# Hybrid encoder step on one core: level-0 masks on VectorE, state-space scaling moved between the delta rule's last solves, first output weights in a free slot

## Chip, cores and metric

One core of a Trainium2 chip. The time is that of one execution of the whole program on the device, in microseconds; the number that counts is the median of several runs. All stretches in the text are on the clock of one profiled execution, counted from the start of its span.

## What is computed

A two-layer encoder step in fp32 over 288 rows: 256 frames of a new stream ("prompt") and 32 frames of a running one ("sample"). Layer 0's mixer runs state-space heads and gated delta-rule heads side by side; layer 1's mixer is another recurrence; each mixer is followed by a mixture of 32 experts. Cut to what the change touches:

```python
def gdn_block(s_mat, inp):                       # delta rule, one block of rows
    ...
    a_mat = (beta[:, :, None, :] * dec_strict * jnp.einsum('bthk,bshk->btsh', k, k)).transpose(0, 3, 1, 2)
    eg = jnp.exp(gam)
    rhs = beta[..., None] * (v - eg[..., None] * jnp.einsum('bthk,bhkv->bthv', k, s_mat))
    u = lax.linalg.triangular_solve(a_mat + jnp.eye(l), rhs, left_side=True, lower=True, unit_diagonal=True)
    qk = jnp.einsum('bthk,bshk->bhts', q, k) * dec_incl.transpose(0, 3, 1, 2)
    o = jnp.einsum('bhts,bhsv->bthv', qk, u) + eg[..., None] * jnp.einsum('bthk,bhkv->bthv', q, s_mat)
    tail = jnp.exp(gam[:, -1:, :] - gam)
    s_new = s_mat * jnp.exp(gam[:, -1])[:, :, None, None] + jnp.einsum('bshk,bsh,bhsv->bhkv', k, tail, u)

def ab_mixer(...):
    ...
    y = rms_norm(y * silu(z_s), by 2 groups)               # state-space half, 1024 channels
    o = rms_norm(o, w['gdn_norm'][j]) * jax.nn.silu(z_g)   # delta-rule half, 1024 channels
    mix = jnp.concatenate([y, o], axis=-1) @ w['w_out_ab'][j]
```

## The kernel before

The 288 rows are three tiles of 128, 128 and 32 rows (tiles 0 and 1 are the prompt, tile 2 the sample). Each engine has its own program written out by hand, and semaphores order them; each runs its program strictly in order. SP issues the transfers, also in order.

The stage around the change comes behind the state-space heads. For each tile the delta rule's triangular matrix is inverted by levels: VectorE cuts the 32-wide diagonal blocks into a compact matrix (`gdn_mats`, L1127), GpSimd masks it for level 0 and, in one operation, for levels 1 to 4 (`gdn_masked`, L523 and L525), TensorE does level 0 (`gdn_first`, L1692) and for each further level a product (L1708, L1715) and an update (L1727 to L1737), with copies on ScalarE (`gdn_p`) and sums on VectorE (`gdn_level`). GpSimd further scales the far blocks (`gdn_far`, L537, L539), copies diagonal blocks (`gdn_blocks`) and makes two side products, the scaled queries and keys (`gdn_sides`, L551, L552). The levels of the three tiles are interleaved by hand on every engine. Then per tile TensorE does a product with the known state (`gdn_known`, L1751), a solve (`gdn_solve`, L1767) and an output with the state's update (`gdn_output`, L1783 to L1787); VectorE makes the right-hand side (`gdn_rhs`), scales the solution (`gdn_solved`) and updates the state (`gdn_state`); ScalarE copies the output out of PSUM (`gdn_out`, L771).

The state-space half waits meanwhile in `cat[:, 0:8]`. TensorE sums its squares (L1845) between `gdn_known(2)` and `gdn_output(1)`, ScalarE takes the root, and VectorE scales the half by the root and by a weight (`ssd_scale`, two operations over 128 x 2304) as its last step of the stage, behind `gdn_state(2)`. Then `head_norm` normalises the delta-rule half in three rounds of heads: ScalarE squares (L814), TensorE sums (`round_sums`, L1858), ScalarE roots, VectorE scales. The output projection (`project_out`, L1890, L1895) takes 16 chunks of 128 channels in four groups of four, each with 2 MB of weights: groups 0 and 1 are the state-space half, groups 2 and 3 the delta-rule half. The weights come into three ring slots, which hold delta-rule data before, so SP loads them behind the last state store (L404 to L411). VectorE adds the result to the residual; then the expert stage begins, whose first expert's weights SP loads once the mixer's output is complete (`cat_ready` 3).

```python
            gdn_update(2, 4)
            gdn_solve(1)
            gdn_known(2)
            ...
            gdn_output(1)
            gdn_solve(2)
            gdn_output(2)
```

Of the kernel before, what the change touches and what calls it, by code (L numbers as in the profile page):

```python
# [8 lines left out]
P = 128  # L9
KD = D_MODEL // P  # L10
TILES = 3
# [16 lines left out]
GROUP = 512  # L28
# [16 lines left out]
SUB = 32  # L45
INNER = 5
# [33 lines left out]
def build(nc, ins, outs):  # L80
# [9 lines left out]
    with ctx:  # L90
# [8 lines left out]
        xn = sb("xn", [P, TILES, D_MODEL])  # L99
# [90 lines left out]
        for three in (gDQK, gDKK):  # L190
            three.append(take(cur, SSD_DEAD, 8, SUB))
        gQ2 = take(cur, SSD_DEAD, 8, SUB)
# [23 lines left out]
        gKtok = in_uT_early(4, P)  # L216
# [119 lines left out]
        for name in ("x_loaded consts_loaded h_ready sq_done xn_ready xnT_ps uT_ready dve_step act_step "  # L336
                     "proj_ps proj_evac conv_out conv_act small_ps small_evac sp_exp1 sp_pos sp_ln g_ready "
                     "ea_ready cum_ps cum_ready pool_step ssd_in ssd_diff ssd_exp ssd_w ssd_y ssd_upd st_T st_Tevac z_act "
                     "state_in ssd_final yg_ready sq2_done nrm_ps nrm_done gdn_in gdn_diff gdn_exp gdn_mats "
                     "gdn_gb gdn_vt gdn_c gdn_far gdn_dqk gdn_copied gdn_masks "  # L340
                     "gdn_bm gdn_p gdn_pe gdn_pt gdn_tu gdn_ks gdn_rhs gdn_u gdn_ue gdn_o gdn_upd gdn_out "
                     "state_loaded gdn_vb gdn_side cat_ready out_ps out_loaded0 out_loaded1 out_loaded2 "
                     "states_out conv_new_ready beta_ready ring0 ring1 ring2 decay_in decay_act hg_keep hg_d "
                     "hg_e hg_qk hg_att hg_acc hg_in hg_x hg_y hg_ex hg_upd hg_tr hg_out lg_ps rt_diff rt_exp "
                     "rt_A rt_R rt_OH rt_tab route_done xn_stored xg_zero xgathered weight_ready "
                     "xg_T xT_ready wg0 wg1 wg2 wu0 wu1 wu2 wd0 wd1 wd2 gu_ps sg_ready hid_ready "
                     "hT_ps hidT_ready y_ps y_ready placed_ps h_added y_out hist_loaded ss_set small_loaded "
                     "final_loaded rs_done").split():
            s_(name)
# [19 lines left out]
        def _(sp):  # L369
# [32 lines left out]
            for n, name in enumerate(("gdn_p", "gdn_s")):  # L402
# [4 lines left out]
            def load_out(src, groups, first):  # L407
                for g in range(groups):
                    if g >= 3:
                        sp.wait_ge(S["out_ps"], first + g - 2)  # L410
                    sp.dma_start(ring[g % 3].rearrange("p a b -> p (a b)").rearrange("p (c d) -> p c d", c=4),  # L411
                                 src[g * 4 * P:(g + 1) * 4 * P, :].rearrange("(c p) d -> p c d", p=P)
                                 ).then_inc(S[f"out_loaded{g % 3}"], 16)

            sp.wait_ge(S["yg_ready"], 2)
            load_out(ins["w_out_ab"], 4, 0)
# [41 lines left out]

            sp.wait_ge(S["cat_ready"], 3)
# [16 lines left out]
            load_out(ins["w_out_c"], 2, 4)  # L476
# [16 lines left out]
        def _(pool):  # L493
# [34 lines left out]

            def gdn_far(i):

                s = i % 2
                nb = lambda q, w: gNb[q, i].unsqueeze(2).to_broadcast([w, 8, w])
                pool.wait_ge(S["gdn_mats"], i + 1)
                pool.wait_ge(S["gdn_bm"], 2 * i + 2)
                for r in (0, 2):
                    q, c = slice(SUB * r, SUB * r + SUB), slice(SUB * r + SUB, SUB * r + 2 * SUB)
                    p(G.tensor_tensor(gDKK[s][q, :, c], gDKK[s][q, :, c], nb(q, SUB), ALU.mult))  # L537
                q, c = slice(0, 2 * SUB), slice(2 * SUB, P)
                G.tensor_tensor(gDKK[s][q, :, c], gDKK[s][q, :, c], nb(q, 2 * SUB), ALU.mult).then_inc(S["gdn_far"], 1)  # L539

            def gdn_sides(i):
# [4 lines left out]
                if i:  # L546
                    pool.wait_ge(S["gdn_copied"], i)
                else:
                    pool.wait_ge(S["gdn_far"], 1)
# [3 lines left out]
                                gKtok[0:L].unsqueeze(2).to_broadcast([L, 4, 2, P]),  # L553
# [3 lines left out]
            def gdn_blocks(i):  # L557
# [3 lines left out]
                if i:  # L561
                    pool.wait_ge(S["gdn_bm"], 6)
                else:
                    pool.wait_ge(S["gdn_far"], 2)
# [61 lines left out]
        def _(act):  # L626
# [290 lines left out]
        def _(dve):  # L917
# [209 lines left out]
            def gdn_mats(i):  # L1127
# [10 lines left out]
                c_.then_inc(S["gdn_c"], 1)  # L1138

# [366 lines left out]
        def _(pe):  # L1506
# [178 lines left out]
            def gdn_first(i):  # L1685

                pe.wait_ge(S["gdn_bm"], 2 * i + 1)
# [7 lines left out]
            def gdn_product(i, n):  # L1695
# [3 lines left out]
                if n == 1:  # L1699
                    pe.wait_ge(S["gdn_bm"], 2 * i + 2)  # L1700
# [138 lines left out]
            gdn_solve(1)  # L1839
            gdn_known(2)  # L1840

# [4 lines left out]
            m_.then_inc(S["nrm_ps"], 1)  # L1846
            gdn_output(1)
# [31 lines left out]
            round_sums(0, 0)  # L1879

            def project_out(src, groups, first, between):
                for g in range(groups):
                    pe.wait_ge(S[f"out_loaded{g % 3}"], 16 * out_use(first, g))
                    w = ring[g % 3].rearrange("p a b -> p (a b)").rearrange("p (c d) -> p c d", c=4)
# [14 lines left out]
            pe.wait_ge(S["nrm_done"], 3)  # L1899
            project_out(cat, 4, 0, out_steps_0)  # L1900
# [197 lines left out]
def inv_step(i, n):  # L2098

    return INVERSE.index((i, n))  # L2100
# [108 lines left out]
```

## Time and profile before

| | us |
|---|---|
| median of 3 runs | 1781.13 (1779.69 to 1784.95) |
| the profiled execution, its own time | 1776.18 |
| its span, first to last instruction | 1774.4 |
| TensorE matmuls busy | 1253.9 (71%) |
| VectorE busy | 453.2 (26%) |
| ScalarE busy | 371.4 (21%) |
| GpSimd busy | 65.5 (4%) |

PE is TensorE's matmuls, PEld its weight loads, DVE VectorE, ACT ScalarE, POOL GpSimd, SPq the transfers that SP issues. An element-wise VectorE operation shows line 928, that of a helper, so tensors and shapes tell which one it is. `ps` is PSUM; `arena`, `uT`, `xn` and `cvt` are SBUF. Most matmuls are fp32 and show as two records each. The clock is the share of full TensorE speed that the chip granted. Busy shares are means over stages with different limits; what a stage is worth is read from the chain in that stage.

### The profile page before, as it was taken

How to read it: one execution, taken by the hardware profiler on the slowest of the kernel's cores; microseconds unless marked ns; L12 is line 12 of the kernel's file. 1: busy time of each engine (PE TensorE's matmuls, PEld its weight loads, DVE VectorE, ACT ScalarE, POOL GpSimd, SP SyncE). 2: the span in 40 equal slices, each digit the busy share in tenths (PEclk: the TensorE clock that was granted, in tenths of full speed). 3: DMA queues.
4: the chain of work that ended last, by engine and by line, in shares of the span. 5: the costliest groups of instructions: out<-in, count | busy, mean ns of one | idle time of the engine just before them, and what ended most of it. 6: DMA issues, size and time to landing. Idle time of an engine off the chain costs nothing.

```text
span 1774.4 us, 26723 instructions
## 1 busy us (share of the span) xinstructions
PE 1253.9 (71%) x12028; PEld 830.3 (47%) x12028; DVE 453.2 (26%) x819; ACT 371.4 (21%) x756; POOL 65.5 (4%) x69
## 2 busy tenths in 40 slices
PE   6999976869747556646665799988466655664664
PEld 5777766844434233323332578774343323332332
DVE  3546444320241011101100248611511101110111
ACT  3352121131102111111111233523121111111112
POOL 0000023100000000000000001100000000000000
PEclk9999986759769788888888899988688888788888
DMA  6333010036469999999999141033879999999993
GB/s 251 105 133 109 1 37 4 2 116 239 172 250 423 420 421 419 421 419 420 420 422 411 59 142 48 1 119 113 351 279 421 421 422 420 420 421 419 421 420 152
DMA packets 72540, 473.23 MB, mean 267 GB/s; under 512 B 5600, under 2 KB 15072, under 8 KB 53600
## 3 DMA queue, kind: packets, MB, share of 16 engines
q1 hardware_dynamic: 70112, 466.68, 64.7%
q0 software_dynamic: 2304, 4.72, 0.8%
q8 instruction: 99, 1.62, 0.4%
q14 instruction: 25, 0.20, 0.0%
HBM read 468.28 MB, written 6.77 MB: 268 GB/s over the span
## 4 chain that ended last, share of the span: by engine, by line
PE 51%; DMA 30%; DVE 7%; SPq 5%; issue 3%; ACT 2%; DVEq 0%; POOL 0%; ACTq 0%; POOLq 0%
DMA arena<-in_wu 25%; PE ps L1530 16%; PE ps L1940 9%; SPq L428 5%; PE ps L1890 5%; PE ps L1969 4%; DMA arena<-in_wg 4%; DVE arena L928 3%; PE ps L1959 2%; PE ps L2046 1%; DVE h L928 1%; PE ps L1518 1%; PE ps L1906 1%; PE ps L1895 1%; PE ps L1567 1%
## 5 line engine op out<-in xcount | busy, mean ns | idle before, releaser
L1530 PE MATMUL ps<-uT,arena 128*128 128x288 f32 x1216 | 306.8, 412 | 0.8 <-DVE uT L928 0.8
L1940 PE MATMUL ps<-arena,xn 128*32 128x256 f32 x2048 | 167.0, 496 | 154.7 <-issue 116.0
L1530 PEld LDWEIGHTS ps<-uT,arena 128*128 128x128 f32 x1216 | 232.6, 193 | 66.1 <-issue 2.2
L1940 PE MATMUL ps<-arena,uT 128*32 128x256 f32 x2048 | 163.3, 487 | 122.9 <-issue 87.1
L928 DVE TENSOR_TENSOR uT<-uT,ps 64x256 f32<-64x256 f32 (+1 forms) x72 | 30.2, 424 | 746.1 <-ACT uT L834 677.9
L1940 PEld LDWEIGHTS ps<-arena,xn 128*32 128x32 f32 x2048 | 90.3, 141 | 233.7 <-issue 218.1
L1940 PEld LDWEIGHTS ps<-arena,uT 128*32 128x32 f32 x2048 | 91.9, 139 | 194.5 <-issue 178.2
L1959 PE MATMUL ps<-arena,uT 128*32 128x256 f32 x2048 | 125.2, 385 | 21.6 <-issue 18.6
L843 ACT ACTIVATE xn<-ps 32x256 f32<-32x256 f32 x256 | 95.9, 374 | 199.3 <-PE ps L1959 106.9
L834 ACT ACTIVATE uT<-ps 64x256 f32<-64x256 f32 x64 | 24.0, 375 | 494.6 <-PE ps L1940 494.6
L1969 PE MATMUL ps<-xn,uT 128*128 128x512 f32 (+1 forms) x192 | 92.9, 609 | 18.9 <-DVE h L928 15.6
L928 DVE TENSOR_TENSOR h<-h,ps 128x1024 f32<-128x1024 f32 (+2 forms) x60 | 66.3, 1110 | 148.0 <-PE ps L1969 91.8
L1959 PEld LDWEIGHTS ps<-arena,uT 128*32 128x32 f32 x2048 | 69.7, 110 | 63.6 <-issue 34.3
L1890 PE MATMUL ps<-arena 128*128 128x512 f32 x192 | 87.7, 614 | 3.8 <-DMA arena<-in_w_out_ab 3.8
L928 DVE TENSOR_TENSOR arena<-arena 128x512 f32<-128x512 f32 (+7 forms) x108 | 76.0, 747 | 52.1 <-ACT arena L637 22.1
L1890 PEld LDWEIGHTS ps<-arena 128*128 128x128 f32 x192 | 37.6, 198 | 50.4 <-issue 49.8
L1969 PEld LDWEIGHTS ps<-xn,uT 128*128 128x128 f32 (+1 forms) x192 | 28.7, 162 | 58.2 <-issue 33.8
L1948 PE MATMUL ps<-con,uT 64*128 64x64 f32 x128 | 21.4, 247 | 38.9 <-DVE uT L928 38.9
L1518 PE MATMUL ps<-con,xn 128*128 128x128 f32 (+1 forms) x96 | 18.4, 373 | 41.2 <-DVE xn L939 41.2
L1948 PEld LDWEIGHTS ps<-con,uT 64*128 64x128 f32 x128 | 12.6, 137 | 68.6 <-DVE uT L928 56.2
L1022 DVE SCALAR_TENSOR_TENSOR cvt<-arena,vec,cvt 128x291 f32<-128x291 f32 x84 | 43.9, 523 | 3.0
L2046 PE MATMUL ps<-arena 128*128 128x128 f32 (+1 forms) x352 | 39.0, 270 | 7.6 <-DVE arena L928 7.6
(328 smaller groups left out, 1175.5 us busy)
## 6 DMA issues: line engine op xcount, KB each, us to landing
arena<-in_wg SPq DMA_DIRECT2D x64, 2048.0 KB, 34.3
arena<-in_wu SPq DMA_DIRECT2D x64, 2048.0 KB, 31.0
arena<-in_wd SPq DMA_DIRECT2D x64, 2048.0 KB, 34.7
arena<-in_wA SPq DMA_DIRECT2D x11, 2048.0 KB, 8.4
arena<-in_wC SPq DMA_DIRECT2D x8, 2048.0 KB, 8.7
arena<-in_w_out_ab SPq DMA_DIRECT2D x4, 2048.0 KB, 10.2
arena<-in_w_out_c SPq DMA_DIRECT2D x2, 2048.0 KB, 12.6
xn_rows<-xn SPq DMA_DIRECT2D x4, 512.0 KB, 15.3
```

What stands on the lines that cost most here:

```text
L428: sp.dma_start(dst, src).then_inc(signals[name], 16)
L843: y_ = nc.scalar.activation(yb[SLOTS * q:SLOTS * (q + 1), 256 * g:256 * (g + 1)], ps[SLOTS * g:SLOTS * (g + 1), 5, 0:256], ACT.Copy)
L928: return V.tensor_tensor(out, a, b, op)
L1022: op = V.scalar_tensor_tensor(out, xpad[:, t, j:j + XW], wv(j), out, ALU.mult, ALU.add)
L1518: t_ = nc.tensor.transpose(bank(4 + k % 4, 4, P)[:, j, 0:L], xn[0:L, i, 4 * c + j::KD], ident[0:L, 0:L])
L1530: m_ = MM(ps[:, banks[t % len(banks)], 0:TOK], ring[s][:, k, (t % 4) * P:(t % 4 + 1) * P], uT[:, k, :], start=(k == 0), stop=(k == KD - 1))
L1890: MM(ps[:, 2 * i + n, :], src[:, k, AT[i]:AT[i] + P], w[:, c, 512 * n:512 * n + 512], start=(k == 0), stop=(k == 4 * groups - 1))
L1940: m_ = MM(ps[SLOTS * g:SLOTS * (g + 1), 2 + n % 2, 0:H2], x[:, k, SLOTS * q:SLOTS * (q + 1)], w[s][:, k, H2 * (g % 2):H2 * (g % 2 + 1)], s ...
L1948: t_ = nc.tensor.transpose(bank(4, 2, 2 * SLOTS)[:, m, :], hid[2 * SLOTS:, m * P:(m + 1) * P], ident[2 * SLOTS:, 2 * SLOTS:])
L1959: m_ = MM(ps[SLOTS * g:SLOTS * (g + 1), 5, 0:n_], hidT[:, m, SLOTS * src:SLOTS * (src + 1)], wdb[s][:, k, n_ * g:n_ * (g + 1)], start=(k = ...
L1969: m_ = MM(ps[0:L, b + g, 0:n_], weight[:, AT[t]:AT[t] + L], yb[:, n_ * g:n_ * (g + 1)], start=True, stop=True)
L2046: m_ = MM(bank(step_bank(m), 8, P, n=2)[0:L, hd, 0:L], a_, b_, start=True, stop=True)
```

## The change

- The level-0 mask moves from GpSimd to VectorE, right behind the compact matrix; GpSimd keeps levels 1 to 4. A new semaphore `gdn_b0` releases `gdn_first`.
- GpSimd's program is reordered: the mask of tile 1 waits for the far blocks of tile 0, the mask of tile 2 moves ahead of the side products of tile 0, and these ahead of the block copies of tile 1. The keys that the side products read get a second buffer, so ScalarE's copy no longer waits for the tile before.
- On TensorE the state-space sums move ahead of `gdn_solve(1)`; on VectorE `ssd_scale` moves ahead of `gdn_state(1)`.
- SP loads the first group of output weights into a slot of its own (`w_first`, over dead state-space data), once the last level and the side products are done; groups 1 and 2 once the last output is done; group 3 behind the last state store. Loading the first expert waits for group 0 to be used.
- The output projection starts without the first round of head sums; the rounds move to its chunks (0, 2), (1, 0) and (1, 2). It waits for the copy of the last delta-rule output.
- Two small tensors of tile 2 move to other free memory.

```diff
+        w_first = at(RING, KD, GROUP)
...
-        gKtok = in_uT_early(4, P)
+        gKtok = [in_uT_early(4, P), xn[:, 0, 0:512].rearrange("p (a b) -> p a b", a=4)]
...
+            sp.wait_ge(S["gdn_pe"], len(PRODUCTS))
+            sp.wait_ge(S["gdn_pt"], len(INVERSE))
+            sp.wait_ge(S["gdn_tu"], inv_step(1, INNER + 1) + 1)
+            sp.wait_ge(S["gdn_side"], TILES)
+            load_rows(w_first, ins["w_out_ab"], 0, S["out_loaded0"])
+            store_state(0, "gdn_p")
+            sp.wait_ge(S["gdn_o"], TILES)
+            load_rows(ring[1], ins["w_out_ab"], 1, S["out_loaded1"])
+            load_rows(ring[2], ins["w_out_ab"], 2, S["out_loaded2"])
+            store_state(1, "gdn_s")
             sp.wait_ge(S["states_out"], 16 * 6)
...
-            sp.wait_ge(S["yg_ready"], 2)
-            load_out(ins["w_out_ab"], 4, 0)
+            load_rows(ring[0], ins["w_out_ab"], 3, S["out_loaded0"])
...
+            sp.wait_ge(S["out_ps"], 1)
             sp.wait_ge(S["cat_ready"], 3)
             load_expert(0, 0, None, slots[0])
...
                 if i == 1:
+                    pool.wait_ge(S["gdn_far"], 1)
                     pool.wait_ge(S["states_out"], 64)
+                elif i == 2:
+                    pool.wait_ge(S["gdn_copied"], 1)
                 low = gDc[i][0:L].unsqueeze(1)
-                G.tensor_tensor(gB[i][0:L, 0:1], low, cmask[0:L, 0:1].unsqueeze(2).to_broadcast([L, 1, 8, SUB]), ALU.mult
-                                ).then_inc(S["gdn_bm"], 1)
                 G.tensor_tensor(gB[i][0:L, 1:INNER], low.to_broadcast([L, INNER - 1, 8, SUB]),
...
             gdn_masked(0)
             gdn_far(0)
-            gdn_sides(0)
             gdn_masked(1)
             gdn_far(1)
             gdn_blocks(0)
+            gdn_masked(2)
+            gdn_sides(0)
+            gdn_blocks(1)
             gdn_sides(1)
-            gdn_masked(2)
-            gdn_blocks(1)
             gdn_sides(2)
...
-                if i:
-                    act.wait_ge(S["gdn_side"], i)
-                nc.scalar.activation(gKtok[0:L], bank(7, 4, P)[0:L], ACT.Copy)
+                need(act, S["gdn_side"], i - 1)
+                nc.scalar.activation(gKtok[s][0:L], bank(7, 4, P)[0:L], ACT.Copy)
...
                 c_.then_inc(S["gdn_c"], 1)
+                dve.wait_ge(S["gdn_c"], i + 1)
+                if i == 0:
+                    dve.wait_ge(S["gdn_masks"], 1)
+                elif i == 1:
+                    dve.wait_ge(S["states_out"], 64)
+                tt(gB[i][0:L, 0], gDc[i][0:L], bc(cmask[0:L, 0].unsqueeze(1), 8, SUB), ALU.mult).then_inc(S["gdn_b0"], 1)
...
             gdn_rhs(2)
+            ssd_scale()
             gdn_state(1)
             gdn_solved(2)
             gdn_state(2)
-            ssd_scale()
...
             gdn_update(2, 4)
-            gdn_solve(1)
-            gdn_known(2)
-
+            pe.wait_ge(S["gdn_tu"], inv_step(1, INNER + 1) + 1)
             pe.wait_ge(S["sq2_done"], 3)
             for g in range(2):
                 for c in range(4):
                     m_ = MM(ps[:, g, 0:TOK], ones, Z[:, 4 * g + c, :], start=(c == 0), stop=(c == 3))
             m_.then_inc(S["nrm_ps"], 1)
+            gdn_solve(1)
+            gdn_known(2)
+
             gdn_output(1)
...
                 if (g, c) == (0, 2):
+                    round_sums(0, 0)
+                elif (g, c) == (1, 0):
                     round_sums(0, 1)
-                elif (g, c) == (1, 1):
+                elif (g, c) == (1, 2):
                     round_sums(0, 2)
...
-            round_sums(0, 0)
-
...
             pe.wait_ge(S["nrm_done"], 3)
+            pe.wait_ge(S["gdn_out"], TILES)
             project_out(cat, 4, 0, out_steps_0)
```

## Rows read from the trace of the kernel before

**Rows 1.** The first expert stage by stretch: length, busy time by engine, clock, DMA share.
```profile
core 0: us, PE busy (x) PEld busy (x) DVE busy (x) ACT busy (x) POOL busy (x), PEclk, DMA share, GB/s
467.00:960.00 493.00, 296.18 (x3372) 167.31 (x3372) 73.21 (x159) 72.58 (x195) 9.07 (x9) 0.80 0.98 403
```

**Rows 2.** The chain of waits of the whole run: start us, us, what.
```profile
376.06 3.72 PE ps L1787 x16
...
384.79 2.56 DVE arena L928
387.46 7.90 DMA arena<-in_w_out_ab
395.49 8.97 PE ps L1890 x16
...
463.07 2.67 DVE h L928 x3
```

**Rows 3.** GpSimd's timeline: start us, us, operation [idle before <-releaser].
```profile
263.93 2.18 POOL L551 TENSOR_TENSOR arena<-arena 128x1024 f32<-128x1024 f32 x1 [0.17 <-POOL arena L539]
266.07 1.90 POOL L552 TENSOR_TENSOR arena<-uT,arena 128x1024 f32<-128x1024 f32 x1
...
344.88 1.89 POOL L552 TENSOR_TENSOR arena<-uT,arena 32x1024 f32<-32x1024 f32 x1
```

**Rows 4.** DMA issues: count, KB each, median us from issue to landing.
```profile
arena<-in_w_out_ab SPq DMA_DIRECT2D x4, 2048.0 KB, 10.2
```

**Rows 5.** Timeline of TensorE, VectorE and ScalarE, tiles 1 and 2 up to the seam.
```profile
349.92 4.15 PE L1845 MATMUL ps<-arena,con 128*128 128x288 f32 x16
351.47 1.21 DVE L928 TENSOR_TENSOR arena<-arena 32x1024 f32<-32x1024 f32 x1
354.11 0.74 ACT L636 ACTIVATE xn<-ps,con 128x576 f32<-128x576 f32 x1 [8.70 <-PE ps L1845]
356.16 0.68 ACT L637 ACTIVATE xn<-xn 128x576 f32<-128x576 f32 x1
359.46 1.22 DVE L928 TENSOR_TENSOR arena<-arena 128x1024 f32<-128x1024 f32 x1 [6.78 <-PE ps L1787]
362.09 3.59 PE L1767 MATMUL ps<-arena 32*32 32x128 f32 x16 [2.66 <-DVE arena L928]
...
379.81 0.38 ACT L771 ACTIVATE arena<-ps 128x256 f32<-128x256 f32 x1 [15.88 <-PE ps L1787]
...
382.20 2.55 DVE L928 TENSOR_TENSOR arena<-arena,xn 128x2304 f32<-128x2304 f32 x1
```

**Rows 6.** Timeline of TensorE in the output projection: one round of head sums.
```profile
404.30 1.62 PE L1858 MATMUL ps<-uT,con 128*128 128x288 f32 x6
```

**Rows 7.** The chain of waits inside the delta-rule stage: start us, us, what.
```profile
255.99 0.73 POOL arena L523
...
325.24 1.98 PE ps L1783 x16
```

**Rows 8.** Timeline of VectorE and GpSimd around tile 0's masks.
```profile
254.13 1.71 DVE L928 TENSOR_TENSOR uT<-arena 32x256 f32<-32x256 f32 x4
256.67 2.34 POOL L525 TENSOR_TENSOR arena<-uT,cvt 128x1024 f32<-128x1024 f32 x1
257.91 0.42 DVE L928 TENSOR_TENSOR uT<-ps,cvt 128x256 f32<-128x256 f32 x1 [0.82 <-PE ps L1692]
258.25 1.04 DVE L928 TENSOR_TENSOR uT<-arena,cvt 128x256 f32<-128x256 f32 x1
```

**Rows 9.** Stretches of tile 1's end, the last solve and the projection, columns as in rows 1.
```profile
348.00:360.00 12.00, 11.43 (x81) 10.14 (x80) 4.34 (x5) 3.25 (x4) 0.00 (x0) 1.00 0.00 0
362.00:380.00 18.00, 16.37 (x64) 14.04 (x64) 1.41 (x2) 2.12 (x2) 0.00 (x0) 0.50 0.11 30
395.00:399.00 4.00, 3.51 (x4) 1.51 (x5) 2.18 (x2) 1.28 (x1) 0.00 (x0) 0.50 1.02 414
399.00:463.00 64.00, 64.00 (x263) 28.90 (x261) 3.75 (x4) 7.18 (x7) 0.00 (x0) 1.00 0.43 167
```

More of the change, by code:

```diff
@@ L189, in build @@
         compact = [None, [take(cur, SSD_DEAD, 8, SUB) for _ in range(4)], None]
-        for three in (gDQK, gDKK):
-            three.append(take(cur, SSD_DEAD, 8, SUB))
-        gQ2 = take(cur, SSD_DEAD, 8, SUB)
+        gDKK.append(take(cur, SSD_DEAD, 8, SUB))
+        in_xn = lambda at_: xn[:, 2, at_:at_ + 8 * SUB].rearrange("p (a b) -> p a b", a=8)
+        gDQK.append(in_xn(280))
+        gQ2 = in_xn(536)
+        w_first = at(RING, KD, GROUP)
         cur = [in_pad]
@@ L339, in build @@
                      "state_in ssd_final yg_ready sq2_done nrm_ps nrm_done gdn_in gdn_diff gdn_exp gdn_mats "
-                     "gdn_gb gdn_vt gdn_c gdn_far gdn_dqk gdn_copied gdn_masks "
+                     "gdn_gb gdn_vt gdn_c gdn_far gdn_b0 gdn_dqk gdn_copied gdn_masks "
                      "gdn_bm gdn_p gdn_pe gdn_pt gdn_tu gdn_ks gdn_rhs gdn_u gdn_ue gdn_o gdn_upd gdn_out "
@@ L401, in _, with load_rows, store_state @@
             sp.dma_start(GS[1], ins["st_gdn"].rearrange("h k v -> k h v")).then_inc(S["state_loaded"], 16)
-            for n, name in enumerate(("gdn_p", "gdn_s")):
+            def load_rows(dst, src, g, done):
+                sp.dma_start(dst.rearrange("p a b -> p (a b)").rearrange("p (c d) -> p c d", c=4),
+                             src[g * 4 * P:(g + 1) * 4 * P, :].rearrange("(c p) d -> p c d", p=P)).then_inc(done, 16)
+            def store_state(n, name):
                 sp.wait_ge(S["gdn_upd"], 2 + n)
                 sp.dma_start(outs[name].rearrange("h k v -> k h v"), GS[n]).then_inc(S["states_out"], 16)
-            sp.wait_ge(S["states_out"], 16 * 6)
[L407 to L413, printed above, removed]
-            sp.wait_ge(S["yg_ready"], 2)
-            load_out(ins["w_out_ab"], 4, 0)
+            sp.wait_ge(S["gdn_pe"], len(PRODUCTS))
[8 more added lines that the diff above has]
+            store_state(1, "gdn_s")
+            sp.wait_ge(S["states_out"], 16 * 6)
+            load_rows(ring[0], ins["w_out_ab"], 3, S["out_loaded0"])
             def load_expert(s, e, free, signals):
@@ L475, in _ @@
             sp.dma_start(hS[1], ins["st_hgrn"].rearrange("h k v -> k h v")).then_inc(S["state_loaded"], 16)
-            load_out(ins["w_out_c"], 2, 4)
+            for g in range(2):
+                load_rows(ring[g], ins["w_out_c"], g, S[f"out_loaded{g}"])
             for n, name in enumerate(("hgrn_p", "hgrn_s")):
@@ L533, in gdn_far @@
                 pool.wait_ge(S["gdn_mats"], i + 1)
-                pool.wait_ge(S["gdn_bm"], 2 * i + 2)
+                pool.wait_ge(S["gdn_bm"], i + 1)
                 for r in (0, 2):
@@ L546, in gdn_sides @@
                 if i:
-                    pool.wait_ge(S["gdn_copied"], i)
-                else:
-                    pool.wait_ge(S["gdn_far"], 1)
+                    pool.wait_ge(S["gdn_copied"], 2)
                 q4 = gQ[i].rearrange("p (a b) c -> p a b c", b=2)[:, :, :, 0:L]
@@ L552, in gdn_sides @@
                 G.tensor_tensor(gKt[s][0:L].rearrange("p (a b) c -> p a b c", b=2),
-                                gKtok[0:L].unsqueeze(2).to_broadcast([L, 4, 2, P]),
+                                gKtok[s][0:L].unsqueeze(2).to_broadcast([L, 4, 2, P]),
                                 gTail[i][0:L].rearrange("p (a b) -> p a b", b=2).unsqueeze(3).to_broadcast([L, 4, 2, P]),
@@ L561, in gdn_blocks @@
                 if i:
-                    pool.wait_ge(S["gdn_bm"], 6)
+                    pool.wait_ge(S["gdn_side"], 1)
                 else:
@@ L1685, in gdn_first @@
             def gdn_first(i):
-                pe.wait_ge(S["gdn_bm"], 2 * i + 1)
+                pe.wait_ge(S["gdn_b0"], i + 1)
                 if i == 0:
@@ L1699, in gdn_product @@
                 if n == 1:
-                    pe.wait_ge(S["gdn_bm"], 2 * i + 2)
+                    pe.wait_ge(S["gdn_bm"], i + 1)
                 if n == INNER:
@@ L1883, in project_out @@
                     pe.wait_ge(S[f"out_loaded{g % 3}"], 16 * out_use(first, g))
-                    w = ring[g % 3].rearrange("p a b -> p (a b)").rearrange("p (c d) -> p c d", c=4)
+                    w = (w_first if (first, g) == (0, 0) else ring[g % 3]).rearrange("p a b -> p (a b)").rearrange("p (c d) -> p c d", c=4)
                     for c in range(4):
```

## The prediction

> **What bounds the kernel now.** I read three views first: the chain of waits of the whole run, to see on which stage the end hangs; the same chain with the timeline in the delta-rule stage; and the stretches with the granted clock. A projection, a recurrent mixer and an expert stage follow one another twice. The first expert stage is a stream of weights: from 467 to 960 us the DMA engines are busy 0.98 of the time [rows 1]. It opens once the first mixer's residual is done (VectorE at 463.07 [rows 2]), so a microsecond saved before 463 should be a microsecond of the run, and one lost there likewise. All that the change touches lies between 250 and 463 us.
>
> There the reader is to see one seam. TensorE finishes the last delta-rule output at 379.78 (376.06 + 3.72). VectorE then updates the state and scales the state-space half, the last step of it 2.56 us from 384.79; a fetch of the output weights takes 7.90; and only at 395.49 does the output projection start [rows 2]. TensorE then works without a break to 463.
>
> **The change, part by part.** All sums are on the trace's clock.
>
> *The seam.* The scaling moves ahead of the last state updates, and the first 2 MB of weights get a place that is free earlier, so the 395.49 - 379.78 = 15.7 us between output and projection fall away. Three things must hold.
> - Weights: SP issues group 0 after four waits, of which GpSimd's third side product comes last, at 344.88 + 1.89 = 346.8 [rows 3]. The state store behind it on the queue waits for tile 1's update, which is later, so nothing is held up. A load takes 10.2 us in the median [rows 4]: there near 357, some 25 us early. Groups 1 and 2 are issued when the last output is done, near 381.5; group 1 is wanted behind group 0's matmuls and sums, near 401. Group 3 waits for the last state store and is wanted near 436. All hidden; group 0, if it were not, would cost the 7.90 again.
> - Scaling: 2.55 + 2.56 = 5.1 us [rows 2, 5]. VectorE idles 6.78 us ahead of tile 1's state update [rows 5], while output 1 runs. The root that it needs took ScalarE from 354.11 to 356.84 (356.16 + 0.68) behind the sums [rows 5]; with the sums two TensorE steps earlier it ends near 353. So scaling starts with output 1 and takes 5.1 against 5.4 us: hidden with 0.3 us to spare. Without that cover it would delay the update and the last solve, at most by its own length.
> - The projection gets a wait for ScalarE's copy of the last output out of PSUM: 0.38 us [rows 5], with the handoff +0.5. The rest of TensorE's program is queued behind it.
>
> *Head sums.* The first of three rounds stood in the seam and is now inside group 0. A round of six costs 1.62 us at full clock [rows 6], double that at half: +1.6, as the clock was up by then before. Its squares are ready 3.4 us after the last output (update 2.5, square 0.9), while two chunks of group 0 take 6.9 or more: no wait. The later rounds each get half a group or more for the root and norm before them. Nothing.
>
> *A cover that goes.* The state-space sums (4.15 us from 349.92) stood between the product with the known state and output 1. They hid VectorE's right-hand side of tile 2, two operations of 1.21 us of which the second ends at 351.47 + 1.21 = 352.68 [rows 5], and output 1 waits for it. The sums now stand ahead of solve 1. TensorE's work up to that point is the same, but output 1 meets the wait: 352.68 - 349.99 = +2.7. Solve 2 and output 2 are queued behind, so it all moves the seam.
>
> *Level-0 masks.* GpSimd's mask is a piece of the chain at all three tiles; the first of the three pieces, 0.73 us, stands for them [rows 7]. VectorE does that shape in 0.42 us [rows 8] and saves a handoff between engines: from the compact matrix (254.13 + 1.71 = 255.84) to the mask's end (256.72) 0.88 us become about 0.5. I take 0.35 a tile, -1.0 in all. The masks of levels 1 to 4 start up to 0.7 us earlier on GpSimd. Other bound: VectorE's mask shares its start with GpSimd's big one (2.34 us), and VectorE's add with both inputs in SBUF took 1.04 us beside that, 0.42 with one in PSUM [rows 8]; at 1.04 the masks cost 0.2 to 0.3 us a tile, +0.8. I stay with 0.42, since VectorE has the shorter way to its own result.
>
> The Trainium skill, SBUF — State Buffer, section "Who interferes with whom", says that a VectorE instruction with two SBUF inputs and a GpSimd instruction that reads SBUF exclude each other: the one that issues first runs, the other fully blocks. That speaks against this move. The trace agrees: the 1.04 us add ended at 259.29, just after GpSimd's mask at 259.01.
>
> *GpSimd's order.* Side products of tile 0 (2.18 + 1.90 us [rows 3]) now follow the mask of tile 2, near 308 to 312; output 0 wants them at 325.24 [rows 7]. Those of tile 1 follow the copies of tile 1 and end near 330; output 1 wants them at 357. The second key buffer takes a wait off ScalarE that bound nothing. Nothing; without these margins each would cost at most its own 4.1 us.
>
> *Clock.* TensorE was granted 1.00 (2.4 GHz) from 348 to 360, 0.50 (1.2 GHz) from 362 to 380 and still in the projection's first 4 us, then 1.00 [rows 9]. I take the same levels for the same work, so the projection keeps its slow start (4 us at half speed, 2 us lost). Bounds: a start at full clock gives 2.0; output 1, which now starts after 2.7 us of idling, costs at half clock up to its 5.4 us again.
>
> **Sum.** -15.7 + 0.5 + 1.6 + 2.7 - 1.0 = -11.9 us. The profiled execution took 1776.18 us (span 1774.4), so it would be 1764.3. It lies 5 us below the median of the runs, 1781.13 (1779.69 to 1784.95); the same difference on the median gives **1769.2 us**.
>
> **Rivals.**
> - *Half clock at output 1.* For it: after the idle 2.66 us before solve 2 at 362.09 [rows 5] the clock was down for 18 us [rows 9], and the new gap is as long. Against it: the new gap stands behind 5 us or more of dense matmuls. Between nothing and 5.4 us, say 4: -7.9, 1773.2. Chance 0.17.
> - *GpSimd gets in first.* One VectorE operation releases both masks; if GpSimd's large one starts first and holds VectorE's for its 2.34 us, the mask of tile 0 ends near 258.7 instead of 256.72. Some +2.0 for -0.35 at each tile, +7.0 in all: -4.9, 1776.2. For it: the 1.04 us add. Against it: GpSimd started 0.15 us after the compact matrix, and VectorE follows itself in some 0.03. Chance 0.12. The skill's rule in the section named above makes this the case in which GpSimd issues first.
> - *The change does not reach the seam*: the projection still meets the 7.90 us fetch, -4.0, 1777.1. For that SP would have to stand somewhere behind 347 for 30 us; I find no such wait. Chance 0.04.
> - *Slower: the projection stays at half clock.* For it: from 362 to 380 TensorE was busy 16.37 of 18 us and got 0.50 all the same [rows 9], and the projection now follows straight on. Against it: after 4 us of the same matmuls it had 1.00. A microsecond at half clock loses half of one, so the gain is gone once the low stretch lasts 4 + 2 x 11.9 = 28 us. If two groups (15.8 us each at full clock) run so: +31.6 - 2.0 - 11.9 = +17.7, 1798.8. Chance 0.03.
>
> **How the numbers follow.** The forecast has what is left, 0.64. Its own bounds are 1769.2 - 2.0 (start at full clock) - 1.4 (the lowest run under the median) = 1765.8 and 1769.2 + 1.8 (masks at +0.8) + 1.4 = 1772.4. The range goes on to the clock rival and to GpSimd's, and a little lower for a clock that also stays up in solve 2: 1764.0 to 1776.5. A measurement of this kernel tells 0.3%, 5.3 us, from no change. Faster than 1775.8: the forecast, the clock rival and part of GpSimd's, 0.86. Within 5.3 us: the rest of that and the unreached seam, 0.11. Slower: the projection at half clock, 0.03.
>
> **What would show it.** Right: the first projection matmul less than 1 us after the last output matmul; group 0's weights issued near 347; both scaling operations beside output 1; some 2.7 us of idle TensorE ahead of output 1, released by VectorE; masks of 0.42 us on VectorE; the residual near 451 instead of 463. Wrong: masks of 2 us or more; group 0's first matmul released by a transfer; a group that takes 28 us; an expert stage of more than its 493 us [rows 1], which would give the gain back.

## The result, and the profile after

The changed kernel was timed three times, each time beside the kernel before on the same chip:

| measurement | changed, us: median (range, runs) | before, us | ratio, 95% interval |
|---|---|---|---|
| first | 1766.22 (1763.03 to 1768.73, 4) | 1780.46 | 0.9910 [0.9894, 0.9927] |
| second | 1770.62 (1766.16 to 1779.38, 12) | 1781.26 | 0.9941 [0.9926, 0.9957] |
| third | 1770.16 (1765.45 to 1776.37, 8) | 1781.98 | 0.9942 [0.9920, 0.9963] |

It is faster by 14.2, 10.6 and 11.8 us; the forecast of 11.9 us is a ratio of 1769.2 / 1781.13 = 0.9933. The first profiled execution after the change took 1767.64 us (span 1765.8, granted clock 0.845), against 1776.18 (span 1774.4).

**The seam.** The chain of waits of the changed kernel (start us, us, what), where [rows 2] had 15.7 us between output and projection:

```profile
383.09 3.71 PE ps L1802 x16
386.80 0.52 issue
387.31 8.84 PE ps L1906 x16
396.16 1.46 PE ps L1874 x6
397.61 6.87 PE ps L1906 x16
...
454.29 1.91 PE ps L1911 x32
456.20 0.02 issue
456.22 2.67 DVE h L937 x3
```

L1802 is the last output's state update, L1906 the projection: 0.52 us lie between them, which is the handoff with ScalarE's copy. The first round of head sums (L1874) stands inside group 0 and waits for nothing. The residual starts at 456.22 instead of 463.07.

**Tile 1's end, output 1, the last solve.** Timeline of the changed kernel, all engines, picked rows in order of time (start us, us, engine, line, operation; in brackets the idle time before it and what ended it):

```profile
348.23 6.62 PE L1858 MATMUL ps<-arena,con 128*128 128x288 f32 x16
348.76 1.89 POOL L562 TENSOR_TENSOR arena<-uT,arena 32x1024 f32<-32x1024 f32 x1
350.74 0.38 SPq L406 DMA_DIRECT2D arena<-in_w_out_ab  x1
354.69 1.95 PE L1782 MATMUL ps<-arena 128*128 128x128 f32 x16
356.56 1.93 PE L1766 MATMUL ps<-arena 128*32 128x128 f32 x16
359.98 1.21 DVE L937 TENSOR_TENSOR arena<-arena 32x1024 f32<-32x1024 f32 x1
361.12 2.54 DVE L937 TENSOR_TENSOR arena<-arena,xn 128x2304 f32<-128x2304 f32 x1
361.44 0.46 PE L1798 MATMUL ps<-arena 128*128 128x128 f32 x2 [2.95 <-DVE arena L937]
363.69 2.56 DVE L937 TENSOR_TENSOR arena<-arena,vec 128x2304 f32<-128x2304 f32 x1
367.08 1.23 DVE L937 TENSOR_TENSOR arena<-arena 128x1024 f32<-128x1024 f32 x1 [0.83 <-PE ps L1802]
369.70 3.00 PE L1782 MATMUL ps<-arena 32*32 32x128 f32 x16 [2.66 <-DVE arena L937]
386.83 0.38 ACT L780 ACTIVATE arena<-ps 128x256 f32<-128x256 f32 x1 [15.30 <-PE ps L1802]
```

The lost cover is here: output 1 (L1798) idles 2.95 us for VectorE's right-hand side of tile 2, which ends at 361.19. Before there was no such wait [rows 5]. Both scaling operations (361.12 to 366.25) end beside output 1; VectorE then still idles 0.83 us for it, so the scaling is hidden. SP issues group 0 at 350.74, as soon as GpSimd's third side product (L562) ends at 350.65, and 36.6 us before it is wanted. The state-space sums (L1858) take 6.62 us instead of 4.15, the solve behind them 1.95.

**The clock and the expert stage.** Stretches of the changed kernel, columns as in [rows 1]:

```profile
372.00:384.00 12.00, 10.70 (x40) 9.17 (x39) 1.21 (x1) 0.00 (x0) 0.00 (x0) 0.50 0.03 9
387.31:391.30 3.99, 3.98 (x6) 1.70 (x7) 1.97 (x2) 1.84 (x3) 0.00 (x0) 0.56 0.81 271
391.31:456.20 64.89, 64.84 (x268) 29.68 (x266) 5.93 (x6) 13.40 (x13) 0.00 (x0) 1.00 0.49 186
463.00:956.00 493.00, 298.06 (x3392) 165.32 (x3396) 73.14 (x158) 69.97 (x191) 9.07 (x9) 0.81 0.98 406
```

Output 2 runs at half clock (1.2 GHz), as before [rows 9], although TensorE is busy 10.70 of 12 us; the projection has 0.56 in its first 4 us and then 1.00. The expert stage has the same 493 us, clock and DMA share as in [rows 1].

**What hangs on the residual.** In the two profiled executions of the kernel before, the time from the residual's start to the end of the span is 1774.4 - 463.07 = 1311.3 and 1311.2 us; in the three of the changed kernel 1309.6, 1310.5 and 1309.6. Of the nine other profiled kernels below, eight lie between 1309.2 and 1310.8, one at 1306.6. So the run moves with the residual nearly one to one. What lies behind the residual is about 1 us shorter with the change than before; no run here explains that.

### The profile page after: what moved, and what is told of

The parts are those of the page before. It is cut to its first block, busy times and chain, and to the rows that moved or that the text cites. A ratio compares the mean times of both kernels' runs of the same rounds, so it can differ in the third digit from the quotient of the medians.

```text
span 1765.8 us, 26728 instructions
## 1 busy us (share of the span) xinstructions
PE 1256.8 (71%) x12028; PEld 830.2 (47%) x12028; DVE 454.0 (26%) x822; ACT 371.6 (21%) x756; POOL 64.2 (4%) x66
## 4 chain that ended last, share of the span: by engine, by line
PE 52%; DMA 30%; DVE 7%; SPq 5%; issue 4%; ACT 2%; DVEq 0%; ACTq 0%; POOLq 0%
DMA arena<-in_wu 25%; PE ps L1545 17%; PE ps L1957 9%; SPq L437 5%; PE ps L1906 5%; PE ps L1986 4%; DMA arena<-in_wg 4%; DVE arena L937 3%; PE ps L1976 2%; PE ps L2063 1%; DVE h L937 1%; PE ps L1533 1%; PE ps L1874 1%; PE ps L1911 1%; PE ps L1582 1%
## 5 line engine op out<-in xcount | busy, mean ns | idle before, releaser
L1957 PE MATMUL ps<-arena,xn 128*32 128x256 f32 x2048 | 162.8, 486 | 156.6 <-issue 120.6
L1957 PE MATMUL ps<-arena,uT 128*32 128x256 f32 x2048 | 169.2, 500 | 119.0 <-issue 83.8
L1957 PEld LDWEIGHTS ps<-arena,xn 128*32 128x32 f32 x2048 | 89.5, 139 | 232.7 <-issue 215.5
L1957 PEld LDWEIGHTS ps<-arena,uT 128*32 128x32 f32 x2048 | 92.5, 143 | 195.7 <-issue 179.7
L1976 PE MATMUL ps<-arena,uT 128*32 128x256 f32 x2048 | 126.8, 388 | 20.7 <-issue 17.4
L1906 PE MATMUL ps<-arena 128*128 128x512 f32 x192 | 87.4, 612 | 0.5 <-issue 0.5
L1906 PEld LDWEIGHTS ps<-arena 128*128 128x128 f32 x192 | 37.5, 197 | 46.3 <-issue 45.6
## 6 DMA issues: line engine op xcount, KB each, us to landing
arena<-in_w_out_c SPq DMA_DIRECT2D x2, 2048.0 KB, 11.8
```

The costliest lines, as they stand in the source:

```text
L1906: MM(ps[:, 2 * i + n, :], src[:, k, AT[i]:AT[i] + P], w[:, c, 512 * n:512 * n + 512], start=(k == 0), stop=(k == 4 * groups - 1))
L1957: m_ = MM(ps[SLOTS * g:SLOTS * (g + 1), 2 + n % 2, 0:H2], x[:, k, SLOTS * q:SLOTS * (q + 1)], w[s][:, k, H2 * (g % 2):H2 * (g % 2 + 1)], s ...
L1976: m_ = MM(ps[SLOTS * g:SLOTS * (g + 1), 5, 0:n_], hidT[:, m, SLOTS * src:SLOTS * (src + 1)], wdb[s][:, k, n_ * g:n_ * (g + 1)], start=(k = ...
```

## The experiments

**The changed kernel again**, and the kernel before with a profile. No edit.

> The changed kernel once more, on the chip of the runs beside it. Theory (sum of the prediction, 11.9 us saved): ratio to before 0.9933, some 1768. Rival (the delta-rule stage itself costs or gives back several us from one execution to the next through the granted clock): a second trace has the same order of work, the first projection matmul again less than 1 us behind the last output, but the stage from the first state-space transposes to that point differs by 2 us or more from the first trace's 142.2 us (244.66 to 386.83), and where it differs the clock of the stretch differs.

> The kernel before once more, one look. Theory: the projection starts 15.7 us behind the last output again. Rival on the clock (which parts of the delta-rule stage run at the higher clock is settled anew in each execution, whatever the kernel): the stage from the first state-space transposes to the last output takes 2 us more or less than the first trace's 136.9 us (242.92 to 379.81), though nothing was changed; if it is the change that moves the clock, it is the same within 0.5 us.

> The changed kernel once more, beside the two versions with the sums elsewhere and the one with GpSimd's order turned, all on one chip. Two measurements so far gave ratios to before of 0.991 and 0.9941. Theory: the gain is 10 to 16 us, the spread comes from where the half-clock stretches of the delta-rule stage fall in an execution: 0.991 to 0.994, first projection matmul 0.5 us behind the last output, 2.95 us of idling ahead of output 1. Rival: one of the two measurements belonged to its chip, and this one repeats only one of them.

The changed kernel's times are in the table above; the kernel before took 1782.99 us in its one run. What the seam shows is the same every time: 15.7 and 15.8 us before, 0.5 in all three after; output 1 idles 2.95 us in all three. What differs is the stretch of levels ahead of it. From tile 0's solve to the state-space sums the instructions are the same, and they took 27.08, 31.04 and 33.81 us in the second, first and third measurement. Stretches of the second, the first and the third, columns as in [rows 1]:

```profile
319.53:346.61 27.08, 22.89 (x490) 20.81 (x489) 9.70 (x17) 5.20 (x10) 6.39 (x9) 0.88 0.01 2
```

```profile
317.19:348.23 31.04, 26.89 (x491) 24.59 (x489) 9.70 (x17) 5.21 (x10) 6.40 (x9) 0.72 0.01 2
```

```profile
320.02:353.83 33.81, 29.62 (x490) 27.30 (x488) 9.71 (x17) 5.20 (x10) 6.39 (x9) 0.65 0.01 2
```

VectorE, ScalarE and GpSimd are busy for the same time to 0.01 us; TensorE is busy 22.9, 26.9 and 29.6 us at a granted clock of 0.88, 0.72 and 0.65. So one kernel's stage moves by 6.7 us between executions by the clock alone. The first two expectations named 2 us over the whole stage as the sign of this, and neither pair of profiles shows it by itself: 140.4 us against 142.2 in the changed kernel, 138.4 against 136.9 in the kernel before. The third measurement does, with 146.8. Single profiles can't settle terms of 1 or 2 us here; the waits in them can.

**Where the seam's 15.7 us went: weights late, scaling late, both.**

Weights late puts group 0 behind the last output, as groups 1 and 2; scaling late makes it VectorE's last step again.

```diff
-            load_rows(w_first, ins["w_out_ab"], 0, S["out_loaded0"])
             store_state(0, "gdn_p")
             sp.wait_ge(S["gdn_o"], TILES)
+            load_rows(w_first, ins["w_out_ab"], 0, S["out_loaded0"])
...
-            ssd_scale()
             gdn_state(1)
             gdn_solved(2)
             gdn_state(2)
+            ssd_scale()
```

> The first group of output weights is issued only once the last output is done, with groups 1 and 2 behind it; all else as in the changed kernel. Theory (the early slot hides a fetch): the projection starts 7.9 us after the last output instead of 0.5, released by the transfer, and the run is 7 to 8 us slower than the changed kernel. Rival (the fetch was only exposed because the scaling stood in front of it): the projection starts no later than 3 us behind the last output, at most 2 us slower.

> VectorE scales the state-space half behind the last state update again; weights early, sums early as in the changed kernel. Theory (the move of the scaling is worth its own length and the update's): the projection starts 2.5 + 5.1 = 7.6 us behind the last output instead of 0.5, released by VectorE, and the run is about 7 us slower than the changed kernel; solve 2 starts no sooner, as the scaling beside output 1 cost it nothing. Rival (the scaling beside output 1 already delayed the state update and solve 2): solve 2 starts up to 1 us sooner after output 1, and the loss is 6 us or less.

> The changed kernel with the scaling last and the first weights issued only with the last output. Theory (each of the two hides behind the other, as both start when the last output is done): the projection starts about 8 us after the last output, not 15.7 as in the kernel before, and the run is 6 to 8 us slower than the changed kernel, the same as with either part alone. Rival (the two add up, since the projection needs both): 15 us, and with the lost cover slower than the kernel before.

Measured: weights late 1776.26 us, ratio 0.9966 [0.9945, 0.9986]; scaling late 1777.19, 0.9982 [0.9964, 1.0001]; both 1774.71, 0.9960 [0.9944, 0.9975]. The first two were timed beside the changed kernel and are 5.6 and 6.6 us slower than it, a little less than the 7 to 8 expected; the changed kernel was not timed beside the third. Timeline of TensorE at the projection's start, weights late, scaling late, both late:

```profile
399.38 5.94 PE L1906 MATMUL ps<-arena 128*128 128x512 f32 x10 [7.98 <-DMA arena<-in_w_out_ab]
```

```profile
394.43 6.24 PE L1906 MATMUL ps<-arena 128*128 128x512 f32 x7 [7.63 <-DVE arena L937]
```

```profile
391.83 4.60 PE L1906 MATMUL ps<-arena 128*128 128x512 f32 x5 [8.14 <-DMA arena<-in_w_out_ab]
```

Each half alone leaves some 8 us, and so do both together. The fetch (7.98) and the update with the scaling (7.63 = 2.5 + 5.1) are about equally long and, started at the same point, lie beside each other. Before, they stood one behind the other, because SP issued the fetch only behind the scaled half: 7.6 + 7.9 = 15.5 of the 15.7. So half of the seam goes once the fetch starts with the last output's end, and the other half only if both are early. Doing one of the two is worth no more than doing neither and starting the fetch there.

For that it takes the slot of its own as well as the lifted wait. In the kernel before, SP also waits for the last state store ahead of the fetch. Timeline of SP there, and the store's row among the DMA issues (KB, median us from issue to landing):

```profile
382.31 0.37 SPq L404 DMA_DIRECT2D out_gdn_s<-arena  x1
387.46 1.48 SPq L411 DMA_DIRECT2D arena<-in_w_out_ab  x3
```

```profile
out_gdn_s<-arena SPq DMA_DIRECT2D x1, 512.0 KB, 3.2
```

The store landed near 385.5 (382.31 + 3.2), so with only the wait for the scaling lifted the fetch would have started some 2 us earlier, and not 7.6. That is an estimate from these rows; no run tried it.

**The lost cover: the sums back in their place.** The scaling then moves behind `gdn_solved(2)`, since the root comes later.

```diff
-            pe.wait_ge(S["gdn_tu"], inv_step(1, INNER + 1) + 1)
+            gdn_solve(1)
+            gdn_known(2)
             pe.wait_ge(S["sq2_done"], 3)
...
-            gdn_solve(1)
-            gdn_known(2)
             gdn_output(1)
...
-            ssd_scale()
             gdn_state(1)
             gdn_solved(2)
+            ssd_scale()
             gdn_state(2)
```

> The state-space sums stand again between the product with the known state and output 1, and VectorE scales behind the scaled solution of tile 2, beside output 2, where it idles 12.9 us. Theory: the sums cover the right-hand side again, TensorE's idling of 2.95 us ahead of output 1 goes, the projection still starts less than 1 us behind output 2, and the run is about 2.7 to 3 us faster than the changed kernel beside it. Rival 1 (that idling is only moved, to the next solve): output 1 starts sooner, solve 2 no sooner, 0 us. Rival 2 (scaling in the new place delays the last state update and with it the head sums): the first head sums wait, some 2 to 5 us slower.

> The version with the state-space sums back between the known product and output 1 and the scaling behind solve 2's state step, on the same chip. Theory: the lost cover of 2.7 to 2.95 us comes back, and the scaling (5.1 us) still ends before the last output does: 2.5 to 3 us less than the changed kernel. Rival: the later scaling delays the squares of the first head round, and nothing is gained, within 1 us.

Measured: 1767.64 us (0.9931 [0.9906, 0.9956]), 3.0 less than the changed kernel of the same measurement; again 1764.65 (0.9912 [0.9886, 0.9939]), 5.5 less. The order is the expected one both times, though the intervals overlap. The profile shows the cause. Timeline of TensorE in the second of the two:

```profile
348.57 4.15 PE L1860 MATMUL ps<-arena,con 128*128 128x288 f32 x16
352.56 0.39 PE L1798 MATMUL ps<-arena 128*128 128x128 f32 x2
...
360.74 3.58 PE L1782 MATMUL ps<-arena 32*32 32x128 f32 x16 [2.66 <-DVE arena L937]
```

Output 1 follows the sums with no idle time. The seam is 0.5 us here too, so the scaling, which VectorE finishes at 370.63 beside output 2, costs nothing in this place.

**Another place: the sums halved.** Half of them stands where it was, ahead of output 1; the other half goes behind output 1, where TensorE idles 2.66 us ahead of solve 2 in the kernel before and in the changed one. ScalarE takes the root behind tile 1's output copy, and VectorE scales behind `gdn_solved(2)`, as in the two runs above.

```diff
-            pe.wait_ge(S["gdn_tu"], inv_step(1, INNER + 1) + 1)
+            gdn_solve(1)
+            gdn_known(2)
...
+            group_sums(0)
             gdn_output(1)
+            group_sums(1).then_inc(S["nrm_ps"], 1)
             gdn_solve(2)
```

> The state-space sums are cut in two halves of about 2.05 us at full clock: one between the product with the known state and output 1, one between output 1 and solve 2; ScalarE's root follows its copy of output 1, and VectorE scales beside output 2. Theory (each half fits a gap in which TensorE idles, 2.95 and 2.66 us in the changed kernel): idling ahead of output 1 and solve 2 falls below 1 us each, solve 2 starts no later behind output 1 than before, and the run is some 4 us faster than the changed kernel, 1 us faster than with the sums undivided. Rival 1 (the root is now late and the scaling with it): the projection starts more than 1 us behind the last output, no gain over the undivided sums. Rival 2 (fewer gaps keep the granted clock up in solve 2 and output 2): the two take 10 us or less instead of 16, and the gain is 8 us or more.

> The version with the state-space sums halved (one half ahead of output 1, one half ahead of solve 2), measured on the same chip as the changed kernel. Theory: both covers are whole again (idle ahead of output 1 under 1 us instead of 2.95, ahead of solve 2 0.72 instead of 2.66), so 3.5 to 5 us less than the changed kernel of this batch, with a ratio between the two of 0.997 to 0.998. Rival: the 4 to 7 us of the earlier runs were the clock of those executions; then within 1.5 us of the changed kernel.

Measured: 1763.47 us (0.9881 [0.9864, 0.9899]) and 1762.58 (0.9906 [0.9879, 0.9933]), the lowest time in both measurements that it was in, and 7.6 us under the changed kernel of its second one, more than the 3.5 to 5 expected. From the undivided sums in their old place (1764.65 us in the same measurement) the runs do not tell it apart. Timeline of TensorE in the second:

```profile
351.65 2.21 PE L1861 MATMUL ps<-arena,con 128*128 128x288 f32 x8
354.67 0.46 PE L1798 MATMUL ps<-arena 128*128 128x128 f32 x2 [0.81 <-DVE arena L937]
...
360.10 2.11 PE L1861 MATMUL ps<-arena,con 128*128 128x288 f32 x8
362.93 1.90 PE L1782 MATMUL ps<-arena 32*32 32x128 f32 x16 [0.72 <-DVE arena L937]
```

Both idle stretches are filled, 2.95 to 0.81 and 2.66 to 0.72, and solve 2 runs in 1.90 us instead of 3.00, now straight behind busy TensorE. Together (2.1 + 1.9 + 1.1) that is 5.1 us; the rest is within what the clock moved above. The undivided sums fill only the first of the two: in their profile solve 2 still waits 2.66 us.

**The masks back on GpSimd.**

```diff
+                G.tensor_tensor(gB[i][0:L, 0:1], low, cmask[0:L, 0:1].unsqueeze(2).to_broadcast([L, 1, 8, SUB]), ALU.mult
+                                ).then_inc(S["gdn_b0"], 1)
...
-                tt(gB[i][0:L, 0], gDc[i][0:L], bc(cmask[0:L, 0].unsqueeze(1), 8, SUB), ALU.mult).then_inc(S["gdn_b0"], 1)
```

> The changed kernel with the level-0 mask on GpSimd again, ahead of its other masks; all else as changed. Theory (0.35 us a tile on the chain): the first matmul of each tile comes 0.8 to 0.9 us after the compact matrix instead of 0.5, and the run is about 1 us slower than the changed kernel, less than its runs can tell. Rival (VectorE's mask and the adds behind it cost the chain more through the waits on GpSimd than the mask saves): the second add of tile 2's level 0 falls from 3.12 us to about 1.1, and the run is 1 to 2 us faster than the changed kernel.

Measured: 1767.12 us, 0.9914 [0.9901, 0.9928], inside the changed kernel's own three ratios: the time decides nothing. The trace does. Tile 0 in the changed kernel, timeline of VectorE and GpSimd and then the chain of waits (start us, us, what); last, the chain of waits with the masks on GpSimd:

```profile
255.89 1.71 DVE L937 TENSOR_TENSOR uT<-arena 32x256 f32<-32x256 f32 x4
257.63 0.42 DVE L937 TENSOR_TENSOR arena<-uT,cvt 128x256 f32<-128x256 f32 x1
257.75 2.52 POOL L537 TENSOR_TENSOR arena<-uT,cvt 128x1024 f32<-128x1024 f32 x1 [10.72 <-DVE uT L937]
259.60 0.95 DVE L937 TENSOR_TENSOR uT<-arena,cvt 128x256 f32<-128x256 f32 x1
260.41 3.50 POOL L549 TENSOR_TENSOR arena<-arena 32x256 f32<-32x256 f32 x2
```

```profile
257.63 0.44 DVE arena L937
...
258.11 1.12 PE ps L1707 x64
```

```profile
257.87 0.43 DVE uT L939
...
258.44 0.73 POOL arena L537
...
259.21 1.12 PE ps L1703 x64
```

With VectorE's mask the compact matrix ends at 257.60 and TensorE's first product starts at 258.11, 0.5 us later; with GpSimd's it is 258.30 and 259.21, 0.9. So 0.4 us at tile 0; the same difference is 0.35 us at each of the other two (0.5 against 0.85). VectorE's mask took 0.41 to 0.43 us at all three tiles, and GpSimd's big mask started 0.04 to 0.12 us behind it and took 2.5 to 2.6 us instead of 2.34.

**GpSimd's order: tile 0's side products ahead of tile 2's mask again**, with the waits turned to match.

```diff
             gdn_blocks(0)
-            gdn_masked(2)
             gdn_sides(0)
+            gdn_masked(2)
             gdn_blocks(1)
```

> GpSimd's order turned at one place: tile 0's side products (2.2 + 2.1 us) go ahead of tile 2's large mask again, instead of behind it. The changed kernel shows one VectorE addition of tile 2's second level at 3.12 us instead of 1.1, beside the mask and the first side product. Theory: that addition is no longer beside two GpSimd operations in a row, so 0.4 to 1.7 us; but TensorE's next product releases VectorE later than that anyway (1.33 us of idling behind the addition), so the time is the changed kernel's within 1 us, or 1 to 2 us more if the mask, now some 4 us later, is late for tile 2's first product of the inner levels. Rival: the addition is on the path, and the time falls by 1.5 to 2.5 us.

Measured: 1767.75 us, 0.9929 [0.9906, 0.9952], the same as the changed kernel beside it (0.9942) within the intervals. Its median is 2.4 us lower, which by itself would fit the rival; the trace decides. Timeline of VectorE and GpSimd at tile 2, in the changed kernel and with the order turned:

```profile
306.24 2.57 POOL L537 TENSOR_TENSOR arena<-arena,cvt 32x1024 f32<-32x1024 f32 x1 [11.25 <-DVE arena L937]
308.10 3.12 DVE L937 TENSOR_TENSOR arena<-arena,cvt 32x256 f32<-32x256 f32 x1
308.77 2.17 POOL L561 TENSOR_TENSOR arena<-arena 128x1024 f32<-128x1024 f32 x1
312.55 0.68 DVE L1182 COPY arena<-ps 64x512 f32<-64x512 f32 x1 [1.33 <-PE ps L1752]
```

```profile
305.02 2.58 POOL L537 TENSOR_TENSOR arena<-arena,cvt 32x1024 f32<-32x1024 f32 x1 [6.24 <-DVE arena L936]
306.87 1.00 DVE L936 TENSOR_TENSOR arena<-arena,cvt 32x256 f32<-32x256 f32 x1
311.33 0.68 DVE L1181 COPY arena<-ps 64x512 f32<-64x512 f32 x1 [3.45 <-PE ps L1751]
```

The addition falls from 3.12 to 1.00 us and VectorE's idle time behind it grows from 1.33 to 3.45 us, by just as much: TensorE's product sets when VectorE goes on. GpSimd's order changes an operation's length here and not the chain, and the margin is 1.33 us. With the masks on GpSimd in the changed order the same addition took 3.23 us, so it is the order and not the mask's place that makes it long.

## Why the prediction came out

The forecast case was the one that happened. Its steps, each as a mean over the profiled executions, two of the kernel before and three of the changed one; the stage is counted from its first transposes, 242.92 us in the first profile before and 244.66 in the first after:

| stretch | forecast | before | changed | measured |
|---|---|---|---|---|
| first transposes to solve 1, or to the sums now ahead of it | -1.0 (masks) | 102.2 | 104.6 | +2.3 |
| from there to output 1 | +2.7 | 9.5 | 12.9 | +3.4 |
| output 1 to the last output's end | 0 | 25.9 | 25.6 | -0.2 |
| seam | -15.7 + 0.5 | 15.7 | 0.5 | -15.2 |
| projection, to the residual's start | +1.6 | 67.5 | 69.2 | +1.7 |
| sum | -11.9 | | | -8.0 |

With the masks' own 1.1 us (below) in place of the first row, the sum is -11.4, so the forecast of -11.9 came from its terms and not from errors that cancel. The first row is another matter. Stretches of its length in the first profile before and the first after, columns as in [rows 1]:

```profile
242.92:344.35 101.43, 75.40 (x2309) 68.65 (x2309) 45.34 (x74) 24.59 (x43) 30.82 (x32) 0.70 0.07 19
```

```profile
244.66:348.23 103.57, 77.36 (x2309) 70.77 (x2309) 46.15 (x77) 24.49 (x43) 29.51 (x29) 0.70 0.07 18
```

TensorE idled 26.0 us of the first and 26.2 of the second; the other profile before has 26.2, the other two after 25.0 and 24.7. The mean idle time thus fell by 0.8 us, near the forecast of -1.0. The +2.3 comes from TensorE's busy time, which is 3.2 us longer in the mean.

- *The seam* was right, in size and mechanism, and the late versions show that it needed both halves. Group 0's weights were issued 36.6 us before they were wanted, and a load takes 7.8 us in the median of the changed kernel, so they are there some 29 us early, against 25.
- *The lost cover* was right: 2.95 us by the wait, against 2.7. The step "TensorE's work up to that point is the same" left out 0.4 us in the mean: the sums now stand where the clock is still down, 6.62 us instead of 4.15 in the first profile, and the solve behind them gets the full clock, 1.95 instead of some 3.7.
- *Scaling* was hidden, with 0.83 us to spare instead of 0.3.
- *The head sums* inside group 0 were right: no wait, and the projection longer by 1.7 us.
- *The masks* were right: 0.4 us at tile 0 and 0.35 at the others, 1.1 in all. The rival in which GpSimd gets in first falls: VectorE started 0.03 us after its own last operation at every tile of the three profiles, and GpSimd behind it.
- *The rival of half clock at output 1* is half true. In the second profile of the changed kernel output 1 took 7.2 us with its state update instead of 5.6; but solve 2 was then 2.2 us instead of 3.0, so that it cost about 1 us, not 4, and in the other two it did not happen.
- *The residual near 451* was wrong for that execution: 456.22. The step that failed is the one headed clock, "I take the same levels for the same work". Of the 5 us by which it came late, 1.7 lie ahead of the stage (244.66 against 242.92) and 3.1 in the table's first row (103.6 against 101.4, where -1.0 was forecast). That stretch lay between 98.6 and 108.2 us in all fourteen profiled executions, 101.4 and 103.0 with the kernel before, and TensorE's busy time in it, for the same 2309 records, between 73.2 and 83.5 us. It moves with the execution, as the three stretches of one kernel show; whether the change also shifts its mean, two profiles of the kernel before cannot tell. The medians of 4 to 12 runs (-10.6 to -14.2) lie about the sum, and one profile beside one other (span -8.6) does not.
- *"It opens once the first mixer's residual is done"* was too short. The rest of the run follows the residual at a fixed distance, as shown; but from 497 to 511 us DMA's share in the changed kernel is 0.18, and SP's next weight issue, at 511.50, waits 40.8 us for the first expert's products (L1957), which free the slot. The term is not touched by that.
- *The projection at half clock*, the slower rival, did not happen in any of the three profiles of the changed kernel: 0.50 to 0.56 in the first 4 us, and then 0.99 to 1.00.

## What to carry to other kernels

A seam between two stages is often two latencies in a row that only a wait puts in a row: look first for all that the issuing queue waits for, since a fetch that could start with the last output gave half of the gain here. It took a free slot as well as the lifted wait. Work taken from between two dependent steps to make a later stage start earlier may have been the cover of another engine's operation, so read what the other engine does during it; splitting that work over two idle stretches gave the lowest times here, though the runs do not tell it from leaving the work in its old place. Where the clock differs from one execution to the next, compare waits and gaps between profiles, not the ends of stages.

## What the runs showed of the hardware that was not expected

- A VectorE addition with both inputs in SBUF waited through two GpSimd operations in a row. It was issued at 308.10 during GpSimd's mask, which ended at 308.81, and ended at 311.22, just behind the next GpSimd operation (308.77 + 2.17 = 310.94). VectorE did not get its turn between the two; the other two profiles of the changed kernel show 3.13 and 3.15 us. At tile 0 it did: GpSimd's mask ended at 260.27, its next operation started 0.14 us later at 260.41, and VectorE's addition ended at 260.55 after 0.95 us. So it lost its turn only where GpSimd went on without a gap. The Trainium skill, SBUF — State Buffer, section "Who interferes with whom", says that such a pair of instructions shares one read path and that the one which issues first blocks the other fully. The wait for the mask agrees; the wait for the product, which started 0.67 us after the addition, does not follow from that rule.
- GpSimd's mask, started 0.12 us behind VectorE's 0.42 us mask, took 2.52 instead of 2.34 us; VectorE's own was no longer than the operation of that shape with one input in PSUM [rows 8].
- The same 490 TensorE instructions took 22.9 to 29.6 us of busy time in three executions of one kernel, at a mean granted clock of 0.88 to 0.65. What decides it in an execution was not tried.
